# Two fixed experts sharing their passes: a routed expert stage in 11 passes instead of 12

## The reference, cut to what matters

```python
glog = (hf @ w_rg + b_rg).astype(f32)                 # 4 groups of experts
gsel = jnp.argmax(glog, axis=-1)                       # top 1 group
elog = (hf @ w_re + b_re).reshape(c, 4, 4)             # 4 experts in each group
top_v, top_i = lax.top_k(elog_of_gsel, 2)              # top 2 experts in it
wts = jax.nn.softmax(top_v, axis=-1) * gw
a = jnp.einsum('cd,edf->cef', hf, w_gate)              # 1024 -> 256
b = jnp.einsum('cd,edf->cef', hf, w_up)                # 1024 -> 256
act = jax.nn.silu(a) * b * comb[..., None]
return jnp.einsum('cef,efd->cd', act, w_down)          # 256 -> 1024
```

## Time and profile before

| | us |
|---|---|
| median of 3 runs | 797.34 |
| lowest, highest | 795.62, 798.36 |
| span of the profiled execution | 795.5 |
| PE busy in the span | 762.2 (96%) |
| DVE busy | 379.9 (48%) |
| ACT busy | 204.9 (26%) |
| POOL busy | 106.8 (13%) |
| mean DMA rate over the span | 172 GB/s |

### The profile page before, as it was taken

How to read it: one execution, slowest core, us unless ns; L and a number is a source line. 1 busy time by engine, 2 the same in 40 slices (tenths; PEclk the granted TensorE clock), 3 DMA queues, 4 the chain that set the end, 5 groups by cost and what they waited for, 6 DMA issues and landing times.

```text
span 795.5 us, 12983 instructions
## 1 busy us (share of the span) xinstructions
PE 762.2 (96%) x5070; PEld 494.9 (62%) x5070; DVE 379.9 (48%) x850; ACT 204.9 (26%) x485; POOL 106.8 (13%) x160
## 2 busy tenths in 40 slices
PE   8999999999999999889999999999999999998995
PEld 5455588777778788555566775445556564654442
DVE  3269523997232323766624378434732212214865
ACT  3011213112223354654523200134111111123223
POOL 3000006000000311334500100011111101015002
PEclk9999999999999999999999999999999999999998
DMA  9640493841440499200030279003799999996002
GB/s 324 160 126 0 112 278 139 99 133 57 140 97 17 139 233 266 94 1 1 1 120 2 96 216 384 1 14 128 282 407 409 416 418 416 417 373 211 17 14 106
DMA packets 81287, 136.50 MB, mean 172 GB/s; under 512 B 33926, under 2 KB 57546, under 8 KB 77010
## 3 DMA queue, kind: packets, MB, share of 16 engines
q1 hardware_dynamic: 64700, 110.17, 41.7%
q0 software_dynamic: 3728, 13.38, 4.9%
q10 hardware_dynamic: 12798, 12.12, 4.6%
HBM read 116.55 MB, written 21.19 MB: 173 GB/s over the span
## 4 chain that ended last, share of the span: by engine, by line
PE 80%; DMA 8%; DVE 6%; issue 2%; ACT 2%; POOL 1%; DVEq 0%; SPq 0%; POOLq 0%; ACTq 0%
PE ps L1215 29%; PE ps L1300 10%; PE ps L1656 6%; PE ps L1904 5%; PE ps L1788 4%; PE ps L1222 3%; PE ps L1776 3%; DMA merged<-in_w_exp_down 3%; DMA w_slot<-in_w_exp_down 2%; PE ps L1441 2%; PE ps L1820 2%; PE ps L1491 2%; PE ps L1537 2%; PE ps L1518 2%; DMA wgu<-expert_rows,pos_i 1%
## 5 line engine op out<-in xcount | busy, mean ns | idle before, releaser
L1215 PE MATMUL ps<-w_slot,hT 128*128 128x396 f32 (+1 forms) x192 | 71.1, 529 | 0.6 <-DMA w_slot<-in_w_in 0.4
L1215 PE MATMUL ps<-hT,w_slot 128*128 128x288 f32 x256 | 63.1, 407 | 0.0
L1215 PEld LDWEIGHTS ps<-hT,w_slot 128*128 128x128 f32 x256 | 48.3, 190 | 13.9 <-issue 0.8
L1215 PEld LDWEIGHTS ps<-w_slot,hT 128*128 128x128 f32 x192 | 36.1, 190 | 32.5 <-issue 13.4
L2987 DVE SCALAR_TENSOR_TENSOR th<-th,ps 128x256 f32<-128x256 f32 x12 | 5.1, 421 | 103.2 <-ACT th L2248 103.2
L1788 PE MATMUL ps<-w_slot,hT 128*32 128x256 f32 x544 | 49.7, 380 | 0.0
L1300 PE MATMUL ps<-hT,w_slot 128*128 128x288 f32 x144 | 37.3, 407 | 0.0
L1215 PE MATMUL ps<-qg,w_slot 128*128 128x288 f32 x128 | 33.7, 408 | 0.0
L1788 PEld LDWEIGHTS ps<-w_slot,hT 128*32 128x32 f32 x544 | 26.3, 110 | 10.0 <-issue 2.3
L2728 DVE TENSOR_REDUCE nm_p<-ps 128x2 f32<-128x256 f32 (+3 forms) x32 | 25.0, 819 | 15.6 <-PE ps L1491 15.5
L1300 PEld LDWEIGHTS ps<-hT,w_slot 128*128 128x128 f32 x144 | 27.3, 190 | 7.6 <-issue 0.2
(11 more groups left out here) (508 smaller groups left out, 1416.5 us busy)
## 6 DMA issues: line engine op xcount, KB each, us to landing
merged<-in_w_exp_down SPq DMA_DIRECT2D x10, 1024.0 KB, 15.9
w_slot<-in_w_in SPq DMA_DIRECT2D x8, 1024.0 KB, 7.7
wgu<-in_w_exp_gate SPq DMA_DIRECT2D x8, 1024.0 KB, 12.1
wgu<-in_w_exp_up SPq DMA_DIRECT2D x8, 1024.0 KB, 14.1
w_slot<-in_w_exp_gate SPq DMA_DIRECT2D x8, 1024.0 KB
w_slot<-in_w_exp_up SPq DMA_DIRECT2D x8, 1024.0 KB
w_slot<-in_w_exp_down SPq DMA_DIRECT2D x6, 1024.0 KB
expert_rows<-onsaT ACTq DMA_DIRECT2D x12, 512.0 KB, 8.2
```

The costliest lines, as they stand in the source:

```text
L1215: ins = pe.matmul(out, a, b, start=(n == 0), stop=(n == len(pairs) - 1))
```

## The change

The passes become 11. A pass is now written as its four units of 32 slots (`UNITS_OF_PASS`). Expert 0 gets 96 slots instead of 128; expert 1 keeps 96, 32 of them beside expert 0 in pass 0 and 64 in pass 1 beside an ordered expert. Of the ordered experts 3 have 128 slots (4 before), 4 have 96 (5 before) and 7 have 64 (5 before). Two columns of 64 are split over two passes (three before). There are now 8 passes with two experts and 3 with one (7 and 5 before). The list of loads, the tables, the matmuls that make the list by pass and the first list (`idx[:, 0:1]`) follow from that. Pass 0 uses `gate_up_of_two`, which takes over the callback that turns the rows of pass 1.

```diff
-RANK_OF_COLUMN = [0, 1, 6, 2, 7, 8, 3, 9, 10, 4, 14, 5, 11, 12, 13, 15]
-COLUMNS_OF_PASS = [[0], [1, 12], [2, 12], [3], [4, 13], [5, 13], [6], [7, 14], [8, 14], [9], [10, 15], [11]]
-NPASS = len(COLUMNS_OF_PASS)
+RANK_OF_COLUMN = [0, 1, 2, 5, 6, 3, 7, 8, 9, 10, 4, 11, 12, 13, 14, 15]
+UNITS_OF_PASS = [[0, 0, 0, 1], [1, 1, 11, 11], [2] * 4, [3, 3, 3, 12], [4, 4, 4, 12], [5] * 4, [6, 6, 6, 13], [7, 7, 7, 13],
+                 [8, 8, 14, 14], [9, 9, 15, 15], [10] * 4]
+NPASS = len(UNITS_OF_PASS)
 OF_PARITY = [-(-NPASS // 2), NPASS // 2]
-LOADED = [0, 1, 12, 2, 3, 4, 13, 5, 6, 7, 14, 8, 9, 10, 15, 11]
+LOADED = [0, 1, 11, 2, 3, 12, 4, 5, 6, 13, 7, 8, 14, 9, 15, 10]
...
-    loads = [LOADED.index(column) for column in COLUMNS_OF_PASS[n]]
-    own = 2 if COLUMNS_OF_PASS[n][-1] == NE - 1 else 3
-    return [loads[0]] * own + [loads[-1]] * (4 - own)
+    return [LOADED.index(column) for column in UNITS_OF_PASS[n]]
...
                 gate_up_weights(4)
                 gate_up_weights(5)
+                gate_up_weights(6)
                 down_weights(3)
-                gate_up_weights(6)
                 gate_up_weights(7)
                 down_weights(4)
+                down_weights(5)
                 gate_up_weights(8)
-                down_weights(5)
                 down_weights(6)
                 gate_up_weights(9)
+                gate_up_weights(10)
                 down_weights(7)
-                gate_up_weights(10)
                 gate_up_weights(11)
                 down_weights(8)
+                down_weights(9)
                 gate_up_weights(12)
-                down_weights(9)
                 down_weights(10)
                 gate_up_weights(13)
+                gate_up_weights(14)
                 down_weights(11)
-                gate_up_weights(14)
                 gate_up_weights(15)
                 down_weights(12)
                 down_weights(13)
...
                 pe.matmul(out[:, 0:NPASS], ident[:], by_column[:, 0:NPASS], start=True, stop=True)
+                pe.matmul(out[96:P, 0:1], ident[:, 0:32], by_column[:, 1:2], start=True, stop=True)
                 for h in range(2):
-                    pe.matmul(out[96:P, 1 + h:8 + h:3], ident[:, 32 * h:32 * h + 32], by_column[:, 12:15], start=True, stop=True)
-                return pe.matmul(out[64:P, 10:11], ident[:, 0:64], by_column[:, 15:16], start=True, stop=True)
+                    pe.matmul(out[96:P, 3 + h:7 + h:3], ident[:, 32 * h:32 * h + 32], by_column[:, 12:14], start=True, stop=True)
+                pe.matmul(out[0:64, 1:2], ident[:, 32:96], by_column[:, 1:2], start=True, stop=True)
+                pe.matmul(out[64:P, 1:2], ident[:, 0:64], by_column[:, 11:12], start=True, stop=True)
+                return pe.matmul(out[64:P, 8:10], ident[:, 0:64], by_column[:, 14:16], start=True, stop=True)
...
-            def gate_up_of_two(j, n, u):
+            def gate_up_of_two(j, n, u, between=None):
...
-                gate_up(j, 0, 0, lambda: turn_rows(j, 1, 1, 0))
+                gate_up_of_two(j, 0, 0, lambda: turn_rows(j, 1, 1, 0))
...
-            tt(idx[:, 0:1], first_f[:, 0:1], o[:, NE:NE + 1], ALU.add).then_inc(first_made, 1)
+            tt(idx[0:96, 0:1], first_f[0:96, 0:1], o[0:96, NE:NE + 1], ALU.add)
+            tt(idx[96:P, 0:1], first_f[0:32, 1:2], o[0:32, NE + 1:NE + 2], ALU.add).then_inc(first_made, 1)
```

More of the change, by code:

```diff
@@ L61 @@
 MAXR = -(-ROWS // CAP)
-RANK_OF_COLUMN = [0, 1, 6, 2, 7, 8, 3, 9, 10, 4, 14, 5, 11, 12, 13, 15]
-COLUMNS_OF_PASS = [[0], [1, 12], [2, 12], [3], [4, 13], [5, 13], [6], [7, 14], [8, 14], [9], [10, 15], [11]]
-NPASS = len(COLUMNS_OF_PASS)
+RANK_OF_COLUMN = [0, 1, 2, 5, 6, 3, 7, 8, 9, 10, 4, 11, 12, 13, 14, 15]
+UNITS_OF_PASS = [[0, 0, 0, 1], [1, 1, 11, 11], [2] * 4, [3, 3, 3, 12], [4, 4, 4, 12], [5] * 4, [6, 6, 6, 13], [7, 7, 7, 13],
+                 [8, 8, 14, 14], [9, 9, 15, 15], [10] * 4]
+NPASS = len(UNITS_OF_PASS)
 OF_PARITY = [-(-NPASS // 2), NPASS // 2]
-LOADED = [0, 1, 12, 2, 3, 4, 13, 5, 6, 7, 14, 8, 9, 10, 15, 11]
-LAST_PASS = [max(n for n, columns in enumerate(COLUMNS_OF_PASS) if column in columns) for column in LOADED]
+LOADED = [0, 1, 11, 2, 3, 12, 4, 5, 6, 13, 7, 8, 14, 9, 15, 10]
+LAST_PASS = [max(n for n, columns in enumerate(UNITS_OF_PASS) if column in columns) for column in LOADED]
 NX = 4
@@ L1101, in row_of @@
                 pool.iota(out, [[step, out.shape[-1]]], base=first, channel_multiplier=0, allow_small_or_imprecise_dtypes=True)
[L1102 to L1106, removed]
+            pool.memset(base_at[:, 0:1], 0.0)
+            pool.memset(base_at[:, 1:2], 96.0)
+            row_of(base_at[:, 2:NPASS], 2 * CAP, CAP)
+            pool.memset(base_at[:, 11:12], float(CAP + 64))
+            row_of(base_at[:, 12:14], 3 * CAP + 96, 3 * CAP)
+            row_of(base_at[:, 14:16], 8 * CAP + 64, CAP)
+            for at, cap in ((slice(0, 2), 96), (slice(2, 3), 128), (slice(3, 5), 96), (slice(5, 6), 128), (slice(6, 8), 96),
+                            (slice(8, 10), 64), (slice(10, 11), 128), (slice(11, 16), 64)):
                 pool.memset(cap_at[:, at], float(cap))
-            for at, split in ((slice(0, 12), 0), (slice(12, 15), 1), (slice(15, 16), 0)):
+            for at, split in ((slice(0, 12), 0), (slice(12, 14), 1), (slice(14, 16), 0)):
                 pool.memset(split_at[:, at], float(split))
@@ L1112, in _ @@
             row_of(first_at[:, 2:NE], NE - 3, -1)
-            for at in (slice(0, 2), slice(2, 3), slice(3, 4), slice(4, 6), slice(6, 7), slice(7, 9), slice(9, 10), slice(10, 11),
-                       slice(11, 12), slice(12, 15), slice(15, 16)):
+            for at in (slice(0, 3), slice(3, 5), slice(5, 6), slice(6, 10), slice(10, 11), slice(11, 16)):
                 row_of(rank_of[:, at], RANK_OF_COLUMN[at.start], 1)
@@ L1783, in gate_up_of_two @@
                     for k in range(KD):
+                        if w and k == 4 and between:
+                            between()
                         if w == 0 and k % 4 == 0:
@@ L1824, in of_two @@
             def of_two(n):
-                return len(COLUMNS_OF_PASS[n]) == 2
+                return len(set(UNITS_OF_PASS[n])) == 2
             def turn_rows_of_tile0(j):
```

## The result

The changed kernel takes 800.47 us (median of 20 runs, 798.60 to 802.35) against 797.94 us (20 runs, 794.59 to 801.81) for the kernel before: ratio 1.0037, 95% interval 1.0026 to 1.0048, so 3 us slower by the ratio (the medians themselves lie 2.5 us apart). 796.0 was forecast. Its profiled execution took 801.03 us, with a span of 799.3 us.

The account below looks back on a forecast made before the run. PE and the DMA stream together were taken to bound the passes, PE just behind the stream. Span 795.5 - 1.4 (net gain of the end) + 0.1 (before the passes) = 794.2, plus 1.8 to the median: 796.0 us; range 791.0 to 800.5.

Parts of the forecast that it names:

- Steps 1 to 3: The passes: one less saves 11.8 us of PE but 2.5 us of DMA stream; gain 2.5 us, the rest waits.
- Step 4: End of the load list: down weights 14 go out late, so PE waits 1.1 us for weights 15, bounds 0 and 9.9.
- rival D: Last down weights come late: PE waits 9.7 us, the end comes 7.2 us later, 804.5 us; chance 0.12.
- Step 5: After the passes: tile 0 moves 2.5 us earlier, tile 1 less; net gain of the end 1.4 us, bounds 0 and 2.5.
- Step 6: Before the passes: two DVE operations instead of one in the first list add 0.1 us; the added matmuls are hidden.
- B: The pass goes as a whole, PE is the bound and loads keep up: 787.0 us; chance 0.08.
- C: The stream gains more than 2.5 us and the end hides its wait: 4 us faster, 793.3 us; chance 0.16.
- E: Capacities don't hold the rows and the loop runs a second round: about 935 us; chance 0.04.
- A: The forecast itself: passes bound by the stream, part of the gain given back, 796.0 us, 794.0 to 798.3; chance 0.60.

Follow-up runs that it names:

- e6: The kernel before with half of the gate and up weights of experts 4 to 15 not loaded (output not the reference's): 793.99 us.
- e9: The changed kernel with half of the gate and up weights of experts 4 to 15 not loaded and down weights 15 before pg0: 785.13 us.
- e3: The kernel before, 12 passes, with down weights 14 waiting for pass 9's down and pg0 and weights 15 behind them: 802.75 us, ratio 1.0069.
- e5: The changed kernel with half of the gate and up weights of experts 4 to 15 not loaded (output not the reference's): 789.80 us.
- e10: The changed kernel unedited, timed and profiled a second time: 800.91 us, ratio 1.0030 to the kernel before.
- e11: The changed kernel unedited, one more profiled execution: 799.73 us.
- e1: The changed kernel with down weights 15 issued before pg0: 795.94 us, ratio 0.9976 to the kernel before.
- e2: The changed kernel with pg0 issued before down weights 14 and 15: 794.23 us, ratio 0.9958 to the kernel before.
- e4: The kernel before with down weights 15 issued before pg0: 797.01 us, ratio 0.9994.
- e12: The kernel of e2, one more profiled execution: 795.11 us.
- e8: The changed kernel with down weights 12 before gate and up weights 15, and down weights 15 before pg0: 795.17 us, ratio 0.9952 to the kernel before.
- e7: The changed kernel with down weights 12 before gate and up weights 15, and pg0 before down weights 14: 793.95 us, ratio 0.9941 to the kernel before.

## Why the prediction was wrong

It forecast 1.3 us faster; 3 us slower was measured, and it gave that side 0.17.

**Steps 1 to 3, the passes: right.** The pass is worth 11.5 us of PE (e6 against e9; 11.8 forecast), and most of it turned into waits; what shows is 3.2 us where the bytes of the stream gave 2.5. PE's idle time in the stage rose by 5.7 us, and one `gate_up` behind a wait of 2.83 us took 8.80 us instead of 7.11, with a granted clock of 0.50 from 684 to 686 us: together 7.4 where 9 were forecast, at the places named.

**Step 4, the end of the list: this failed.** The prediction put it: "They land at 695.1 + 11.3 + 2.4 = 708.8", "A wait of 1.1 us". The place and the order of events were right: pass 8's `down` frees the slot at the same moment, the engines fall idle (about 4 us, where 1 to 3 were forecast), and weights 14 land in 5.8 us and PE doesn't wait for them. But the term for weights 15 was mis-sized: 17.2 us from the issue of weights 14 to the landing of 15, not 13.7. The queues of the changed kernel from 697.1 to 714.3 us, from the issue to the landing (packets, MB, share of 16 engines), show what was in the way:
```profile
q1 hardware_dynamic: 1685, 4.40, 71.5%
q0 software_dynamic: 230, 0.88, 12.8%
q10 hardware_dynamic: 181, 0.68, 9.6%
```
q0 carries the two gathers of tile 0, 1.05 MB in all, issued at 705.8 and 707.0; q10 the store of pass 8 and the start of that of pass 9, where I had counted one store; q1 has, beside the 4.19 MB counted, a first 0.2 MB of pg1, whose load goes out at 704.05, ahead of the last `down`. The sum had 4.72 MB, 5.96 MB moved. 1.24 MB at 0.416 MB per us are 3.0 us of the error of 3.5, and the gathers are 0.88 MB of it. The other 0.5 us are in the rate, 405 GB/s instead of 416 from 706 to 714 us, and in its rise after the idle stretch. This is a count of bytes: no run left the gathers out. The rule that I used two steps earlier for the stores, that the engines which start the transfers don't have DMA engines of their own (the Trainium skill, "DMA: Bandwidth & Descriptors", "Issuing engines are not separate DMA queues"), holds here too: the shares add up to 94% over a stretch that begins with 2 us of little transfer. I did not carry it to the gathers.

Two smaller things. The Trainium skill gives the fit that stands behind step 4 ("DMA: Bandwidth & Descriptors", "Anatomy of one DMA") for transfers that GpSimd issues. These loads are SP's; alone one took 4.9 us where that fit has 4.4, and the wait that it gives is 0.2 us and not 0.1. And the upper bound of 9.9 us stands beside the 9.7 of rival D for the same case; 9.7 follows from the rows.

A second term was not in the sum. The four matmuls behind the wait take 3.53 us instead of 1.88, with granted clocks of 0.52 and 0.62 in 714 to 718 us. That is 1.65 us more, on the path, and it comes with the wait: it is there at waits of 4.5 us and more (the changed kernel, e3, e5, e10, e11), and in none of the profiles without that wait (the kernel before, e1, e2, e4, e6 to e9, e12). Of the 9.66 us from the last `down` to the turn of tile 0 it is a part, so the whole price of the late list is best read from e3, 5.5 us timed.

**Step 5, tile 0: failed as a consequence.** It was to hang on the store and its gathers and to move 2.5 us ahead. With the last `down` late it hangs on PE's own results: DVE gets the rows at 716.56, and then waits 3.52 us for the last `down` of PE. DVE in the changed kernel:
```profile
716.56 1.29 DVE L3066 SCALAR_TENSOR_TENSOR x<-wgu,wt_j,x 128x1024 f32<-128x1024 f32 x1 [1.72 <-DMA wgu<-expert_rows,pos_i]
721.36 0.69 DVE L2366 TENSOR_TENSOR x<-x,ps 128x512 f32<-128x512 f32 x1 [3.52 <-PE ps L1845]
```
The turn of tile 0 came at 724.02 where 717.7 was forecast, tile 1's at 732.26 where 727 was; 2.6 us of either stand ahead of the passes.

**Step 6, the router's edits:** nothing in the comparison asks for more than the 0.1 us; the scatter ahead of the passes (1.4 and 1.5 us at its two places) is more than ten times as large.

**The rivals.** B (787.0) and C (793.3) are out for the change as it was made; E too, since the page of the profile counts 11 stores of `expert_rows`, one round of 11 passes. D had place and sign, "the last down weights come late", and its mark, a wait of over 4 us at the last `down`, came true with 4.57. It was priced at 7.2 us by the slowest load of a full queue, and held at 0.12 because the queue was empty at the issue. Both ends were too coarse: an empty queue at the issue says nothing of what joins it before the landing. The real case lay between A and D, and there was no case there. That the range held the time, 800.47 under its end of 800.5, is luck: D's tail reached just so far, and the median of e10 (800.91) lies outside.

**What stays open.** From the first `gate_up` on, the three profiles of the changed kernel are 1.2, 1.6 and 2.4 us longer than the one of the kernel before; the timed difference is 3.0 and, in e10, 2.4 us by the ratios. Whether the rest is the two places ahead of the passes falling to the lower clock more often in this kernel, or the scatter of few profiles, the runs don't tell: profiles are few, and the timed runs show no place. They do show a mean granted clock, and time goes with it within one kernel: of 21 runs of the kernel before (beside e5 to e8) the eight at 0.994 and 0.995 took 796.9 us in the mean, the six at 0.989 to 0.991 took 800.3. The profile of the kernel before, at 0.995, is one of the fast ones, so the 3.8 us between the two profiled spans overstate the change.

## What to carry to other kernels

When a stage is bound by its load stream, removing compute moves time only as far as the stream gets shorter with it (3.2 of 11.5 us here), and only if the list of loads is kept full: look at which slot each of the last loads waits for, and put what is free to go (here pg0) ahead of what is not. For a load issued into an empty queue, sum every byte that is issued until it lands, on every queue, gathers and stores included, and not what stands ahead of it at the issue. And let a range have a case between "hidden" and "as late as the worst load"; this wait came out there.

## What the runs showed of the hardware

- A wait of 4.5 to 5.5 us of PE cost 1.6 to 1.9 us more than its length: the next four matmuls of 128x512 took 3.5 to 3.8 us instead of 1.88, in all five profiles that had it and in no other.
- Shorter waits are less regular. Pass 9's `gate_up` took 8.5 to 8.7 us up to the turn of the activations in all seven profiles in which 2.5 to 3.4 us of wait stood ahead of it (the changed kernel, e2, e7, e8, e10 to e12), against 7.05 us behind 0.82 us in e1. But e1's own wait of 3.16 us before pass 8's `down` was followed by full speed (3.57 us), and one of 1.87 us in e8 by eight matmuls of 128x512 in 5.37 us instead of 3.70, at a granted clock of 0.50.
- Where the stream sets the pace such a loss can cost nothing: e1 and e2 have the last `gate_up` 124.96 and 124.73 us after the first, though e2's `gate_up` of pass 9 is 1.7 us slower; its wait at the next `down` is 2.1 us shorter.
- A wait of 1.3 us at 321 us was followed by the lower clock in 6 of 14 profiles and not in 8, with the same work around it: 1.4 us of scatter that belongs to no edit. It was in all three profiles of the changed kernel and not in the one before, and so looked like its doing until e12 showed it in a kernel whose first profile was free of it.
- One core's 16 DMA engines moved 413 GB/s over 96.0 us and 416 over the next 23.4 us, with loads, stores and gathers mixed. After about 4 us with next to nothing to move the rate read 150 GB/s from 698 to 700 us and 334 in the next 2 us. How much of that is the return from idling isn't shown: e2, whose engines were never idle, read 302 GB/s from 696 to 698 us at a share of 1.08.
